# Decay rows masked in memory, and a second buffer for the first direction's diagonal blocks, in a hybrid DeltaNet/SSD layer

## The reference

```python
def gated_delta_chunked(q, k, v, beta, logg, S0, with_output):
    ...
    G = jnp.cumsum(gc, axis=-1)
    tri = jnp.tril(jnp.ones((CHUNK, CHUNK), dtype=bool))
    decay = jnp.where(tri, jnp.exp(jnp.where(tri, G[..., :, None] - G[..., None, :], 0.0)), 0.0)
    lmat = jnp.where(strict, jnp.einsum("cbhid,cbhjd->cbhij", kb, kc) * decay, 0.0)
    uw = lax.linalg.triangular_solve(lmat + jnp.eye(CHUNK, dtype=lmat.dtype), rhs, ...)
    ...
def ssd_chunked(x, dt, A, Bm, Cm, h0, with_output):
    ...
    decay = jnp.where(tri, jnp.exp(jnp.where(tri, Acs[..., :, None] - Acs[..., None, :], 0.0)), 0.0)
    scores = jnp.einsum("cbgin,cbgjn->cbgij", Cc, Bc)[:, :, :, None] * decay
def ec_moe(h, router_w, w_gate, w_up, w_down):
    ...
    gate, idx = lax.top_k(jnp.swapaxes(aff, 1, 2), cap)
    ...
    return jnp.zeros_like(h).at[bidx, idx].add(ye)
```

## Time and profile before

| what | value |
|---|---|
| median of three runs (lowest, highest) | 1323.39 us (1323.25, 1328.37) |
| the profiled execution, own time | 1324.75 us |
| its span on the core | 1323.0 us |
| PE, DVE, ACT, POOL busy, share of the span | 91%, 57%, 32%, 17% |
| DMA | 274 MB, mean 207 GB/s |

### The profile page before, as it was taken

One profiled execution on the slowest core, in us unless ns is written; L12 is line 12 of the kernel. 1 busy time (PEld: TensorE's weight loads), 2 busy tenths in 40 slices (PEclk: granted clock), 3 DMA queues, 4 the chain that ended last, 5 costly groups with the idle time before them and its releaser, 6 DMA issues.

```text
span 1323.0 us, 15648 instructions
## 1 busy us (share of the span) xinstructions
PE 1206.3 (91%) x6022; PEld 683.3 (52%) x6022; DVE 753.2 (57%) x1075; ACT 418.8 (32%) x1062; POOL 229.1 (17%) x203
## 2 busy tenths in 40 slices
PE   4999999999998999979888999991799999999992
PEld 3555545555544554568777744451444444444440
DVE  5298999887935788559888656658300101010116
ACT  5334233213111111667767544431010101010113
POOL 0300000010000011158686200001100101010112
PEclk9999999999998999989999999996899999999996
DMA  9923355442133443367878755526699999999967
GB/s 365 297 80 95 113 181 155 139 154 96 48 117 90 90 97 93 88 193 232 240 227 256 269 205 191 191 80 242 229 334 352 320 352 318 354 316 352 320 220 195
DMA packets 200407, 274.02 MB, mean 207 GB/s; under 512 B 65365, under 2 KB 114510, under 8 KB 200334
## 3 DMA queue, kind: packets, MB, share of 16 engines
q1 hardware_dynamic: 180422, 215.82, 49.8%
q0 software_dynamic: 13840, 50.86, 12.5%
q10 hardware_dynamic: 6072, 6.35, 1.4%
HBM read 221.03 MB, written 51.97 MB: 206 GB/s over the span
## 4 chain that ended last, share of the span: by engine, by line
PE 71%; DVE 14%; DMA 5%; issue 4%; ACT 3%; SPq 2%; POOLq 0%; DVEq 0%; ACTq 0%
PE ps L2143 23%; PE ps L1298 17%; PE ps L1321 8%; PE ps L1251 7%; PE ps L475 2%; DVE arena L2583 2%; DVE arena L2512 2%; DVE arena L2581 2%; DMA arena<-w_in 1%; DMA arena<-ada_w 1%; PE ps L2042 1%; DMA scan_dram<-arena 1%; DVE arena L725 1%; PE ps L1287 1%; PE ps L569 1%
## 5 line engine op out<-in xcount | busy, mean ns | idle before, releaser
L2143 PE MATMUL ps<-arena 128*128 128x512 f32 (+1 forms) x1072 | 425.3, 554 | 4.6 <-DMA arena<-w_in 4.6
L2143 PEld LDWEIGHTS ps<-arena 128*128 128x128 f32 x1072 | 201.8, 191 | 205.5 <-issue 195.6
L1298 PE MATMUL ps<-arena 128*128 128x512 f32 x512 | 225.2, 593 | 1.5 <-DVE arena L1652 0.8
L2512 DVE SCALAR_TENSOR_TENSOR arena<-arena,taps 128x1024 f32<-128x1024 f32 x160 | 207.3, 1296 | 5.5
L1298 PEld LDWEIGHTS ps<-arena 128*128 128x128 f32 x512 | 95.9, 190 | 115.8 <-issue 113.8
L1658 DVE TENSOR_TENSOR arena<-arena,ps 128x512 f32<-128x512 f32 x16 | 11.0, 688 | 215.6 <-PE ps L1298 215.6
L1251 PE MATMUL ps<-arena 128*128 128x512 f32 x256 | 115.5, 597 | 1.3 <-DMA arena<-w_out 0.9
L1321 PE MATMUL ps<-arena 128*128 128x512 f32 x256 | 112.5, 592 | 0.0
L1321 PEld LDWEIGHTS ps<-arena 128*128 128x128 f32 x256 | 47.5, 190 | 54.0 <-issue 54.0
L1251 PEld LDWEIGHTS ps<-arena 128*128 128x128 f32 x256 | 46.5, 190 | 51.8 <-issue 49.5
L1469 ACT ACTIVATE arena<-ps 128x512 f32<-128x512 f32 x16 | 9.6, 598 | 197.6 <-PE ps L1298 197.6
(11 more groups left out here) (352 smaller groups left out, 1552.7 us busy)
## 6 DMA issues: line engine op xcount, KB each, us to landing
arena<-exp_w_gate SPq DMA_DIRECT2D x16, 2048.0 KB, 11.4
arena<-exp_w_up SPq DMA_DIRECT2D x16, 2048.0 KB, 9.4
arena<-exp_w_down SPq DMA_DIRECT2D x16, 2048.0 KB, 10.1
arena<-ada_w POOLq DMA_DIRECT2D x16, 1024.0 KB, 6.6
arena<-w_in SPq DMA_DIRECT2D x28, 512.0 KB, 3.9
arena<-ada_w SPq DMA_DIRECT2D x4, 2048.0 KB, 19.6
arena<-x SPq DMA_DIRECT2D x16, 512.0 KB, 7.3
arena<-g_dram SPq DMA_DIRECT2D x16, 512.0 KB, 5.0
```

Of the source, the lines that this page charges most:

```text
L1298: last = mm(ps[gu_bank[s] + j][:], xsT[s][:, k, :], ew[s][j][:, k, :], start=(k == 0), stop=(k == KD - 1))
L2143: last = mm(ps[3 * (m % 2) + gi][:, 0:w], wring[(m + 1) % NW][:, k, :], hT[:, k, o:o + w], start=(k == 0), stop=(k == KD - 1))
L2512: ins = v.scalar_tensor_tensor(accg, cin_l[ci % 2][:, j // 3:j // 3 + GR, j % 3:j % 3 + GW], tp[:, j:j + 1], accg, ALU.mult, ALU.add)
```

## The change

1. `masked` and both its users go from DVE, before and in the scan. In their place a new tensor `em_dram` holds, for each of the 20 steps, 128 rows of 12 x 128 masked decay values. POOL writes it during the projection: 20 DMAs write the mask (`decay_mask`, runs of 512 B), and when `g_dram` is there 20 more add the broadcast rows to it (`decay_rows`, `accum_op=add`, memory to memory). They are 768 KB each for the 16 latent steps and 256 KB for the four of the context. The masks are issued at `m` = 1 to 5, four at each; the rows at `m` = 7 to 23, each behind a wait for `w_used >= m`: with `w_used` 20 that of step 16, with 21 that of step 17. SP loads `E` and `E8` from `em_dram`; ACT's exponential waits for the load itself.
2. Direction 0 gets a second buffer, `XY[3]`, in a gap of the arena, with one more memset on POOL. Both directions' `load_xy` are issued at the odd steps, for `three` and `four`, behind all the other loads of the step.
3. The first of the last two scatters writes with an index column in which a token that is in both experts is pushed beyond the last row and so skipped; the second no longer waits for it. DVE computes the column with three small instructions at the routing.
4. `bd_out` and `g_out` become two semaphores, and SP's first two `load_e` stand behind the last `tokens_in`.

```diff
         def xy_of(d, n):
-            return XY[0] if d == 0 else XY[1 + n % 2]
+            return XY[(0, 3)[n % 2]] if d == 0 else XY[1 + n % 2]
...
         def decay(act, step):
-            act.wait_ge(sem("s_de"), turn(d, n + 1))
+            act.wait_ge(sem(f"ld_e{d}{n % 2}"), 16 * (n // 2 + 1))
...
-                if lat(nxt):
-                    mask_ssm(nxt)
                 if s % 2 == 0 and two:
                     block_a(two)
                     block_a(three)
-                if s % 2 == 1 and four:
-                    mask_dn(dve, three)
-                    mask_dn(dve, four)
...
             def load_e(step):
-                if n > 0:
-                    sp_.wait_ge(sem("s_de"), turn(d, n))
...
-                sp_.dma_start(flat(e_of(step)), g_dram[r:r + DN_H].rearrange("g p -> (g p)").unsqueeze(0).to_broadcast([P, QK]))\
-                    .then_inc(sem(f"ld_e{d}"), 16)
+                sp_.dma_start(flat(e_of(step)), em_dram[tile_of(step), d, :, 0:QK]).then_inc(sem(f"ld_e{d}{n % 2}"), 16)
...
             def load_xy(step):
-                if d == 0 and n > 0:
-                    sp_.wait_ge(sem("s_xr"), turn(d, n))
+                if n == 1 and d == 0:
+                    sp_.wait_ge(sem("zero"), 5 + DN_H)
+                    sp_.wait_ge(sem("ld_xy0"), 64)
...
-                if two and s % 2 == 0:
-                    load_xy(two)
...
                 if four and s % 2 == 1:
+                    load_xy(three)
                     load_xy(four)
...
+            def decay_mask(step):
+                pool.dma_start(em_dram[t, d].rearrange("p (h n) -> p h n", h=GD)[:, 0:w, :], bh(neg_mask[:, d, :], w))\
+                    .then_inc(sem("em_out"), 16)
+            def decay_rows(step):
+                pool.dma_start(em_dram[t, d, :, 0:w * P], g_dram[r:r + w].rearrange("g p -> (g p)").unsqueeze(0)
+                               .to_broadcast([P, w * P]), accum_op=ALU.add).then_inc(sem("em_out"), 16)
+            def rows_upto(m):
+                return 2 * (m - M_G + 1) if m <= M_G + 1 else min(4 + m - M_G - 1 + (m > M_V0 - 4), 2 * NS)
...
             for i in range(LE):
                 pool.wait_ge(sem("fin"), NL + i + 1)
-                if i > 0:
-                    pool.wait_ge(sem("out_rows"), 16 * i)
+                if i == 0:
+                    pool.wait_ge(sem("route"), 6)
+                    p.indirect_dma_start(out_rows, bass.IndirectOffsetOnAxis(ap=idx_once, axis=0), yr[i], None,
+                                         bounds_check=T - 1, oob_is_err=False).then_inc(sem("out_rows"), 16)
```

More of the change, by code:

```diff
@@ L56, in hybrid_block @@
     bd_dram = dram("bd_dram", (2, 2 * NT * DN_H, P))
+    em_dram = dram("em_dram", (NT, 2, P, GD * P))
     kk_dram = dram("kk_dram", (NT, P, QK))
@@ L324, in hybrid_block @@
             else:
-                at[0] += 2 * L4
+                XY0B = take(2 * L4).rearrange("p (x n) -> p x n", n=P)
             for lst in (kgT, qgT):
@@ L643, in decay8 @@
                 d, n = step
-                act.wait_ge(sem("s_d8"), turn(d, nl(step) + 1))
+                act.wait_ge(sem(f"ld_e8{d}"), 16 * (nl(step) + 1))
                 for h in range(SSM_H):
@@ L875, in pool_scan @@
             pool.wait_ge(sem("w_used"), NM + 1)
+            p.memset(flat(XY[3]), 0.0).then_inc(sem("zero"), 1)
             pool.wait_ge(sem("aux_used"), N_AUX)
@@ L939, in load_e8 @@
                     sp_.wait_ge(sem("s_fc"), turn(d, nl(step)))
[L940 to L942 removed]
+                sp_.dma_start(flat(E8[d]), em_dram[tile_of(step), d, :, QK:GD * P]).then_inc(sem(f"ld_e8{d}"), 16)
             def load_qk(step):
@@ L1949, in late_load, with rows_at @@
                     .then_inc(sem(f"lt_in{b % 2}"), 16)
-            n_late = 0
-            for m in range(NM):
+            def decay_mask(step):
+                d, n = step
+                t, w = tile_of(step), GD if lat(step) else DN_H
+                pool.dma_start(em_dram[t, d].rearrange("p (h n) -> p h n", h=GD)[:, 0:w, :], bh(neg_mask[:, d, :], w))\
+                    .then_inc(sem("em_out"), 16)
+            def decay_rows(step):
+                d, n = step
+                t, w = tile_of(step), GD if lat(step) else DN_H
+                r = (t * 2 + d) * GD
+                pool.dma_start(em_dram[t, d, :, 0:w * P], g_dram[r:r + w].rearrange("g p -> (g p)").unsqueeze(0)
+                               .to_broadcast([P, w * P]), accum_op=ALU.add).then_inc(sem("em_out"), 16)
+            n_late, n_mask, n_rows = 0, 0, 0
+            M_G, M_LAST = 7, 23
+            def rows_upto(m):
+                return 2 * (m - M_G + 1) if m <= M_G + 1 else min(4 + m - M_G - 1 + (m > M_V0 - 4), 2 * NS)
+            def rows_at(m, n_rows):
+                pool.wait_ge(sem("w_used"), m)
+                for step in steps[n_rows:rows_upto(m)]:
+                    decay_rows(step)
+                return rows_upto(m)
+            for m in range(M_Z0 + 1):
                 upto = min(sum(N_LATE[:m]) + 2, NLB)
@@ L1962, in _ @@
                             pool.dma_start(y_zero_t[t, :, h * 512:(h + 1) * 512], zero).then_inc(sem("y_zero"), 16)
+                    pool.wait_ge(sem("c1"), N_C1 - 1)
+                elif m < M_G:
+                    for step in steps[n_mask:4 * m]:
+                        decay_mask(step)
+                    n_mask = 4 * m
+                else:
+                    if m == M_G:
+                        pool.wait_ge(sem("g_out"), 64)
+                        pool.wait_ge(sem("em_out"), 16 * 2 * NS)
+                    n_rows = rows_at(m, n_rows)
             kb, kb1, kbc = square(kb_f), square(kb1_f), square(kbc_f)
@@ L1974, in _ @@
                             channel_multiplier=0).then_inc(sem("c1"), 1)
+            for m in range(M_Z0 + 1, M_LAST + 1):
+                n_rows = rows_at(m, n_rows)
+            assert n_rows == 2 * NS
             pool_scan(pool)
@@ L2593, in _ @@
             for m in range(M_V0, NM - 1):
-                if m == NM - 2:
-                    for step in steps[:2]:
-                        mask_dn(dve, step)
                 conv(m)
```

36 lines of the change are left out of this document (15 added, 21 removed).

## The result

The changed kernel took 1311.36 us in the median of 4 runs (1308.90 to 1313.86), against 1325.74 us for the kernel before: ratio 0.990, 95% interval 0.987 to 0.993. The forecast was worked out from a median of 1323.4 us before, so it spoke of 8.4 us less; against the 1325.74 us timed beside it the change gives 14.4 us. The profiled execution took 1313.04 us with a span of 1311.3 us; before it was 1324.75 us with 1323.0 us.

A forecast was written before the change was run, and what follows sets the result against it. PE sets the projection's pace; in the scan nothing is full and PE waits for block loads and DVE; the end is a chain. 1324.75 - 13.7 (scan) - 2.5 (end) + 8 (front) = 1316.6, median 1.4 lower: 1315 us, range 1304 to 1329.

The forecast's parts named there:

- blocks 8.8, masks 4.5, eg rows -1.0: Scan: gains from block loads and masks less the eg rows' delay; with 1.4 us at the first full pair, 13.7 us less.
- the 8.8 us go whole, if `block_a` keeps up: Scan, second block buffer: loads issued 21 us before use remove all of PE's 8.8 us "issue" wait at `block_near`.
- DVE is not the bound, so only PE's idling counts: Scan, masks off DVE: of their 46.1 us on DVE only PE's 5.0 us wait for `rest` counts; 4.5 us taken.
- More than 14 us needs gaps that the waits don't show.: Scan's steady part: PE's waits total 13.8 us and no PE work goes, so a larger gain needs unseen gaps.
- The eg rows: Scan: block loads ahead of `load_e` and `load_kg` make eg rows 3 us later; 1 us charged, between 0 and 8.8.
- POOL's wait for the eg rows doubled: Scan: sign, with a new PE wait at L475 for POOL, that the eg rows' rival holds; the wait was 17.4 us.
- they take the blocks' place: Scan rival: PE waits for POOL's late `from_k` instead of at `block_near`, 1323 us; chance 0.18 shared with the wrong-wait case.
- the "issue" wait is something else: Scan rival: the wait is not for block loads, so 8.8 + 1.4 us stay, 1324 to 1325 us; within the shared 0.18.
- Two adding transfers, +8: Front: adding DMAs of steps 16 and 17, 4.0 us each, make tile 20's weights about 8 us later; range 2 to 28.
- the adding hides: Front rival: the two adding DMAs don't hold the engines, costing 0 to 3 us, 1308 to 1309 us; chance 0.26.
- slower: Front rival: adding DMAs hold the engines 12 to 14 us each, 1331 to 1335 us; sign `em_dram` landings over 10 us; chance 0.14.
- The end, -2.5: End: the second scatter no longer waits for the first and starts 2.7 us earlier; 2.5 us taken.

The follow-up runs named there:

- f1: The kernel before with only the second block buffer for direction 0, blocks loaded a pair ahead: 1320.38 us, ratio 0.998.
- f2: The changed kernel with the second block buffer undone, masks from memory and changed scatters kept: 1326.10 us, ratio 1.000 to the kernel before.
- g3: Masks from memory and changed scatters without the second block buffer, block writes behind tile 20's weights: 1309.03 us, ratio 0.986 to the kernel before.
- f3: The kernel before with the second block buffer alone and the block writes behind tile 20's weights: 1311.54 us, ratio 0.990.
- f4: The kernel before with only the block writes (`batch_out`) moved behind the issue of tile 20's weights: 1318.22 us, ratio 0.996.
- e1: The changed kernel with adding DMAs two per tile from `w_used` 13 on, the last out before the block writes: 1306.54 us, ratio 0.987 to before.
- g1: The changed kernel with two more 768 KB adding transfers behind the two at tiles 20 and 21: 1317.64 us, ratio 0.993 to before.
- g2: The changed kernel with one of the two adding transfers issued one tile earlier: 1306.57 us, ratio 0.984 to before.
- e4: The changed kernel with both last scatters as before: 1313.56 us, ratio 0.992 to the kernel before.
- g4: The changed kernel with the second scatter again waiting for the first, whose changed form is kept: 1313.76 us, ratio 0.991 to before.
- e2: The changed kernel with the block writes (`batch_out`) put behind the load of tile 20's weights on SP: 1295.78 us, ratio 0.979 to before.
- e3: The changed kernel with adding DMAs two per tile and block writes behind tile 20's weights: 1298.64 us, ratio 0.981 to before.

## Why the prediction was right, and where it was not

- **Faster by the scan, less what the front costs.** Right in its structure: the wait at `block_near` gone, that for `rest` down from 5.0 to 1.5 us (under 1 was forecast), the periods down to 18.1 us (about 19 was forecast), the wait at tile 20 up, and the time within 3.6 us. Of the term "blocks 8.8, masks 4.5, eg rows -1.0" the idle time is 14.3 us where 12.3 stood: 8.8 for the blocks, 3.5 for the masks, nothing lost to the eg rows, and some 2.6 us of a stall at L515 that the kernel before shows and the working left out. The step that failed is the sentence "the 8.8 us go whole, if `block_a` keeps up", together with "DVE is not the bound, so only PE's idling counts". The blocks alone gave 4.3 us of the seven steps, or 0.4 in the other order, and PE then waited 13.1 us for `rest`. The sum was near because both parts were made at once. There is luck in the total too: the scan gave 6.6 us more than its term, the front and the end took 3.7 us of that back, and the change as a whole, 14.4 us by the medians, was well over the 8.4 us forecast. DVE's own row said so: 125.94 us busy in 145.11, which at the 19.0 us a step forecast for PE (133 us) is 95% with the masks still there. Removing the masks was worth not the 5.0 us of its wait but all that the blocks freed as well.
- **"More than 14 us needs gaps that the waits don't show."** Right for the idle time: what goes beyond the two waits is the 2.57 us stall at L515, in that one execution. Incomplete for the span: 4.3 us more came with the granted clock, 0.96 before and 1.00 now. The working had no term for it.
- **The eg rows.** Charged with 1 us, measured at nothing on PE. What was foreseen did happen one step ahead: POOL's wait for them rose from 17.4 us to 37.7 us, and PE waits nowhere for POOL. The sign "POOL's wait for the eg rows doubled" so came true without its consequence. Of the waits from 586 to 713 us:

```profile
POOL arena L821 <- DMA arena<-eg_dram: 37.7, 11, 7.9
```

  The rival that they take the blocks' place did not come, nor the one that the "issue" wait is something else: with the loads issued a pair ahead it vanished in `f1` as well. As for the products beside the masks, here are a DVE group of the kernel before, and then the same group and POOL's of the changed kernel (groups by shape, 578 to 724 us: count, busy us, mean ns, idle before):

```profile
L796 DVE TENSOR_TENSOR arena<-arena 128x512 f32<-128x512 f32 x26 | 20.7, 834 | 0.0
```

```profile
L784 DVE TENSOR_TENSOR arena<-arena 128x512 f32<-128x512 f32 x29 | 28.6, 1023 | 0.0
L823 POOL TENSOR_TENSOR arena<-arena 128x512 f32<-128x512 f32 x17 | 22.3, 1313 | 1.4 <-DMA arena<-eg_dram 0.2
```

  POOL's 1551 ns became 1313 ns. By the Trainium skill (SBUF — State Buffer, "Who interferes with whom") that is to be expected once the DVE instructions with two SBUF inputs go; the trace agrees in the direction. In the seven steps the same product takes 1404 ns with the masks alone gone (`f2`) and 1405 (`g3`), but also 1451 and 1495 ns with the masks still on DVE and the blocks early (`f1`, `f3`), and 1714 in `f4`; so not all of it is the masks. DVE's own product became longer, 1023 ns instead of 834. That isn't owed to the masks going: it is 1007 and 1044 ns with the blocks alone (`f1`, `f3`), 1059 and 913 with the masks alone (`f2`, `g3`), and 840 in `f4`. No run here tells its cause.

- **The masks written to memory, 0.** Right, the share too: 0.94 from 110 to 180 us, where 0.9 was forecast (0.76 from 95 to 301 us), and PE was busy for the same 204.63 us of 206.
- **Two adding transfers, +8.** Right to 0.4 us in the wait (8.36), and in the mechanism: `e1` takes it away, `g1` and `g2` scale it. The rate taken from the earlier trace rows was the right neighbour; with 4.0 us each expected, 3.0 to 5.0 were measured. The rival "the adding hides" is refuted by the landing of 28.0 us, and "slower" by the wait itself, which grew by 4.2 us for each transfer where over 8 was its condition. The sign that the prediction gave for "slower", landings of over 10 us, was no sign: the two transfers in the stretch landed after 10.5 and 13.1 us. What the working missed is one step up: it took 19.8 us "from issue to landing" as given and did not ask why the load was issued at 385 us. The answer, SP standing in `batch_out`, was worth 14.5 us by the ratios (0.990 to 0.979), 16.5 by the two spans.
- **Start of the kernel.** The changed kernel's PE is 1.85 us late before the wait already (383.97 against 382.12 us for the tile ahead of it). From 40 to 50 us the granted clock was 0.83 there and 1.00 before. This is no part of the change: at 1.00 (before, `e4`, `f3`, `g4`) SP starts the block writes at 376.2 to 376.5 us; at 0.83 (the changed kernel, `e1`, `e2`, `f1`, `f2`, `g1`, `g2`) at 378.0 to 378.3, in `g3` at 380.0; and at 0.66 (`e3`, and `f4`, which has the code of before up to there) at 379.6 and 379.7.
- **The end, -2.5.** The 2.7 us of the working are 2.8 (1316.93 less 1314.12). The term is right for the wait (the scatters are 1.46 us apart instead of 4.43) and wrong for the sum: 0.3 us was measured, since 1.3 us are lost in the closing of the program, and 1.4 at the first scatter in this execution.

In sum, by the profiled executions: the scan gave 6.6 us more than forecast and the stretch behind it 0.7, the front cost 1.5 more, and the end gave 2.2 less, which is, but for rounding, the 3.5 us between the forecast and the profiled execution's difference.

## What to carry to other kernels

Two waits of the same engine in the same step are not two prices. Before adding them, put each remaining engine's busy time against the new period. Here DVE was busy for 87% of the old period and would have been for 95% of the new one; it was the next wait. The second edit was then worth far more than its own wait (14.3 us of the seven steps, not 4.5), the first far less (4.3 or 0.4, not 8.8). And where an engine waits for a DMA, read when the DMA could have been issued, not only how long it took: here the load's slot was free 33 us before its issue, the order on the issuing queue held it back, and one moved line gave as much as the change under study.

## What the runs showed of the hardware

- Adding transfers from memory to memory, 768 KB each with a broadcast source, landed 10.0 us after issue in the median (last row), and each delayed a load that was under way beside them by 3.0 to 5.0 us (landings of 20.2, 25.3, 28.0 and 34.0 us with none, one, two and four). Inside a 206 us stretch where the DMA share was 0.76, those issued there and 13.6 MB of plain writes cost PE nothing. Of the changed kernel's page, DMA issues (count, KB each, median us to landing):

```profile
arena<-w_in SPq DMA_DIRECT2D x28, 512.0 KB, 6.1
em_dram<-neg_mask POOLq DMA_DIRECT2D x16, 768.0 KB, 11.4
em_dram<-g_dram POOLq DMA_DIRECT2D x16, 768.0 KB, 10.0
```

- The granted clock was lower where PE stalled more, though not in strict order: the matmuls of the seven steps were busy for 128.18 us at 0.96 with 16.9 us of idling (before), 126.1 to 126.9 us at 0.98 or 0.99 with 11.4 to 14.7 us (`f1` to `f4`, `g3`), and 123.7 to 124.4 us at 1.00 with 2 to 4 us (the kernels with both parts). From 404 to 450 us it was 0.85 with the 12.95 us wait in front, 0.93 with 4.97 us (`e1`), and 1.00 with none (`e2`). But from 500 to 545 us it was 0.92 in `e1` and 1.00 in the changed kernel, with about the same idling.
- Early in the program (40 to 50 us) the granted clock is 1.00, 0.83 or 0.66 from one execution to the next, with one and the same code (before and `f4`: 1.00 and 0.66), and with 0.83 or 0.66 what follows comes 1.5 to 3.8 us later than with 1.00.
- The close of the program, from the last scatter to the end, is 6.1 us in the four programs without the masks in memory and 7.3 to 7.5 us in the ten with them; the cause is open.
